# A decoder trunk on one core: additions moved to GpSimd between the layers, splits put ahead of moves, and a first x tile made without h

## What is computed

```python
for i in range(DEPTH):
    f = swiglu(rmsnorm(h, P['g_f1_pre'][i]), P['w_f1_gate'][i], P['w_f1_up'][i], P['w_f1_down'][i])
    h = h + 0.5 * rmsnorm(f, P['g_f1_post'][i])
    mo, a1, a2, a3 = mixer(rmsnorm(h, P['g_mix_pre'][i]), bpool[i], bsc[i], bcf[i], pos0, P, i)
    h = h + rmsnorm(mo, P['g_mix_post'][i])
    f = swiglu(rmsnorm(h, P['g_f2_pre'][i]), P['w_f2_gate'][i], P['w_f2_up'][i], P['w_f2_down'][i])
    h = h + 0.5 * rmsnorm(f, P['g_f2_post'][i])
    gate = jax.nn.sigmoid(rmsnorm(h, P['g_ple_pre'][i]) @ P['w_ple_gate'][i])
    h = h + rmsnorm((p[i] @ P['w_ple_proj'][i]) * gate, P['g_ple_post'][i])
```

## Time and profile before

| what | value |
|---|---|
| median of three runs | 1541.18 us |
| the three runs | 1539.96, 1541.18, 1541.54 us |
| the profiled execution's own time | 1541.55 us |
| its span in the trace | 1539.9 us |
| busy: TensorE | 1525.8 us (99%) |
| busy: VectorE | 1034.3 us (67%) |
| busy: ScalarE | 720.5 us (47%) |
| busy: GpSimd | 654.0 us (42%) |
| mean granted TensorE clock | 0.995 |

### The profile page before, as it was taken

How to read it: one execution, slowest core, us unless ns; L and a number is a source line. 1 busy time by engine, 2 the same in 40 slices (tenths; PEclk the granted TensorE clock), 3 DMA queues, 4 the chain that set the end, 5 groups by cost and what they waited for, 6 DMA issues and landing times.

```text
span 1539.9 us, 27992 instructions
## 1 busy us (share of the span) xinstructions
PE 1525.8 (99%) x10361; PEld 1518.3 (99%) x10361; DVE 1034.3 (67%) x1589; ACT 720.5 (47%) x1086; POOL 654.0 (42%) x695
## 2 busy tenths in 40 slices
PE   9999999999999999999999999999999999999997
PEld 9999999999999999999999999999999999999997
DVE  7655437999886755533885554389998866555347
ACT  6333336445466433433753334354554664334356
POOL 2855203499331565500147551045973307554012
PEclk9999999999999999999999999999999999999998
DMA  6545432444443544533334454334444335445422
GB/s 220 169 158 181 180 129 83 164 139 163 151 161 110 187 149 151 186 144 117 125 123 166 148 194 177 119 110 138 152 151 163 121 137 187 156 143 188 150 82 82
DMA packets 54281, 229.30 MB, mean 149 GB/s; under 512 B 3776, under 2 KB 6208, under 8 KB 49856
## 3 DMA queue, kind: packets, MB, share of 16 engines
q1 hardware_dynamic: 53632, 226.07, 42.9%
q10 hardware_dynamic: 576, 2.26, 0.4%
HBM read 225.27 MB, written 3.04 MB: 148 GB/s over the span
## 4 chain that ended last, share of the span: by engine, by line
PE 96%; issue 2%; DVE 1%; POOL 1%; ACT 0%; DVEq 0%; POOLq 0%; ACTq 0%
PE ps L504 29%; PE ps L506 29%; PE ps L505 29%; PE ps L546 2%; PE ps L542 2%; PE ps L543 2%; PE ps L668 1%; PE ps L580 1%; PE ps L572 1%; PE ps L571 1%; PE ps L617 0%; PE ps L609 0%; PE ps L636 0%; POOL x_lo L1765 0%; ACT win L1249 0%
## 5 line engine op out<-in xcount | busy, mean ns | idle before, releaser
L1271 DVE TENSOR_TENSOR w_lo_sb<-raw,w_hi_sb 128x1024 fp32r<-128x1024 f32 (+1 forms) x384 | 546.2, 1424 | 219.8 <-ACT w_hi_sb L903 218.9
L903 ACT ACTIVATE w_hi_sb<-raw 128x1024 fp32r<-128x1024 f32 (+1 forms) x384 | 424.7, 1112 | 546.6 <-PE ps L506 445.7
L504 PE MATMUL ps<-x_hi,w_hi_sb 128*128 128x320 f32 x2176 | 674.2, 310 | 0.8 <-DVE w_lo_sb L1271 0.8
L505 PE MATMUL ps<-x_lo,w_hi_sb 128*128 128x320 f32 x2176 | 671.9, 309 | 0.0
L506 PE MATMUL ps<-x_hi,w_lo_sb 128*128 128x320 f32 x2176 | 671.9, 309 | 0.0
L504 PEld LDWEIGHTS ps<-x_hi,w_hi_sb 128*128 128x128 f32 x2176 | 408.5, 188 | 2.7 <-issue 1.3
L505 PEld LDWEIGHTS ps<-x_lo,w_hi_sb 128*128 128x128 f32 x2176 | 408.6, 188 | 0.3
L506 PEld LDWEIGHTS ps<-x_hi,w_lo_sb 128*128 128x128 f32 x2176 | 408.5, 188 | 0.0
L506 PE MATMUL ps<-mid_hi,w_lo_sb 128*128 128x320 f32 x704 | 217.4, 309 | 0.0
L504 PE MATMUL ps<-mid_hi,w_hi_sb 128*128 128x320 f32 x704 | 217.4, 309 | 0.0
L505 PE MATMUL ps<-mid_lo,w_hi_sb 128*128 128x320 f32 x704 | 217.4, 309 | 0.0
(11 more groups left out here) (244 smaller groups left out, 1720.8 us busy)
## 6 DMA issues: line engine op xcount, KB each, us to landing
raw<-in_w_f_up SPq DMA_DIRECT2D x84, 1024.0 KB, 5.3
raw<-in_w_f_dn SPq DMA_DIRECT2D x32, 1408.0 KB, 5.9
raw<-in_w_gate SPq DMA_DIRECT2D x24, 1024.0 KB, 5.3
raw<-in_w_out SPq DMA_DIRECT2D x12, 1024.0 KB, 5.3
...
```

Source lines behind the costliest of these rows:

```text
L504: pe.matmul(out, whi, rhs_hi, start=start, stop=False, skip_group_check=True)
L505: pe.matmul(out, whi, rhs_lo, start=False, stop=False, skip_group_check=True)
L903: act.activation(w_hi_sb[:, j, 0:n], src[:, 0:n], ACT.Copy).then_inc(w_hi, 1)
L1271: dve.tensor_tensor(w_lo_sb[:, j, 0:n], src[:, 0:n], w_hi_sb[:, j, 0:n].bitcast(F32), ALU.subtract).then_inc(w_lo, 1)
```

## The change

It has four parts.

1. In f1_up of both layers the third pair's step is written out (`split_first_step`): each slot's split stands in front of the move, not behind it.
2. At boundaries 0, 1 and 2 of both layers the first x tile is made without h. ScalarE prepares f and h of tile 0 scaled by the gain ahead of time (`first_ahead`, into gb), and VectorE makes x from them with bc (`first_x`), and a second copy that GpSimd reads instead of ScalarE's. h of tile 0, still needed, is computed behind tile 4, and its square moves behind tile 4's. The order of h is now 1, 2, 3, 4, 0, 5, 6, 7 (`CHASE`).
3. Between the layers GpSimd adds the squares of tiles 0 to 6. TensorE's separate sums for tiles 5 and 6 go; the fillers there are 6, 3 and 3 in place of 4, 1, 1, 4 and 3. The splits of the next layer's first two slots change places with the operations around them.
4. At the end GpSimd multiplies a third chunk by the gain, which VectorE finishes last, and TensorE runs fillers between the sums of the chunks.

```diff
+        CHASE = (1, 2, 3, 4, 0, 5, 6, 7)
+        def h_at(n, m):
+            return (CHASE.index(m) if n < 3 else m) + 1
+        AHEAD_F, AHEAD_H = gb[:, 0, :], gb[:, 1, :]
...
                     if name == "post4":
-                        for m in POST4_ALONE:
-                            keep_warm(WARM_ALONE)
-                            pe.wait_ge(squared, v_sq(L, name, m))
...
-                        keep_warm(WARM_SIG)
+                        keep_warm(WARM_ROOT)
...
                 for i, (b, c) in enumerate(CHUNKS):
+                    for _ in range((6, 3, 3, 3, 0)[i]):
+                        pe.matmul(ps[:, 2, 0:T], pw_hi[:, 0:P], p_hi[:, 0:T], start=True, stop=True)
...
+            def first_ahead(L, n, gain):
+                c = cur[:, COL[gain]:COL[gain] + 1]
+                if n != 1:
+                    act.wait_ge(mid_ready, (L * 2 + (1 if n == 0 else 2)) * FT + 2)
+                act.wait_ge(f_out, v_f(L, n, 0))
+                act.activation(AHEAD_F, f[:, 0, :], ACT.Copy, scale=c).then_inc(ahead, 1)
+                act.activation(AHEAD_H, h[:, 0, :], ACT.Copy, scale=c).then_inc(ahead, 1)
...
-                    act.activation(CHASE_SQ[m - 1], h[:, m - 1, :], ACT.Square).then_inc(squared, 1)
+                    while done < DT and (order[done] < m and (n == 3 or order[done] or m > 4)):
+                        act.activation(CHASE_SQ[done], h[:, order[done], :], ACT.Square).then_inc(squared, 1)
+                        done += 1
...
-                    if nxt_layer and m in (5, DT - 1):
-                        split(*nxt_layer, 0 if m == 5 else 2)
+                    if nxt_layer and m == DT - 1:
+                        split(*nxt_layer, 2)
                     sigmoid(sg[:, m % RING3, :], ga[:, m % 2, :], L, "pg", m)
+                    if nxt_layer and m in (5, 6):
+                        split(*nxt_layer, m - 5)
...
+                def first_x():
+                    dve.wait_ge(ahead, (L * 3 + n) * 2 + 2)
+                    dve.tensor_tensor(steps[1], AHEAD_F, bc, ALU.mult).then_inc(x0_step, 1)
+                    dve.wait_ge(x0_step, L * 3 + n + 1)
+                    dve.tensor_tensor(x_hi[:, 0, :], steps[1], AHEAD_H, ALU.add).then_inc(x0_hi, 1)
+                    dve.tensor_tensor(SCALED_H[0], steps[1], AHEAD_H, ALU.add).then_inc(gh_ready, 1)
...
-                step(0)
-                new_h(0)
-                dve.wait_ge(h_ready, before + 1)
-                dve.tensor_scalar(x_hi[:, 0, :], h[:, 0, :], cur[:, g:g + 1], None, ALU.mult).then_inc(x0_hi, 1)
+                if n < 3:
+                    first_x()
...
                     if i - 1 not in POOL_X:
                         x_low(i - 1)
+                    if n < 3 and i == 4:
+                        step(0)
+                        new_h(0)
...
+            def split_first_step(L, ph):
+                for j in range(4):
+                    split(L, ph, 2, j)
+                    dve.wait_ge(halves_done, v_half(L, ph, 1, j) + 4)
+                    if j % 2 == 0:
+                        dve.wait_ge(mid_ready, L * 2 * FT + 2 + j // 2 + 1)
+                    move((ga, gb)[j % 2][:, j // 2, :], j)
...
                 dve.wait_ge(ple_out, L * DT + DT)
+                dve.wait_ge(summed, v_sq(L, "post4", DT - 3))
...
-            for i in (2, 3, 4):
+            for i in (3, 4):
                 b = CHUNKS[i][0]
                 dve.scalar_tensor_tensor(HT[i], HT[i], rinv[:, b:b + 1], G_ROW[i], ALU.mult, ALU.mult).then_inc(y_dve, 1)
+            dve.wait_ge(hg_ready, 3)
+            b = CHUNKS[2][0]
+            dve.tensor_scalar(HG[2], HG[2], rinv[:, b:b + 1], None, ALU.mult).then_inc(y_dve, 1)
...
                 if L + 1 < DEPTH:
+                    for m in range(DT - 1):
+                        wait_alone(squared, v_sq(L, "post4", m))
+                        if m == 0:
+                            pool.tensor_copy(ssq[:, 0:T], sq[:, 0, :]).then_inc(summed, 1)
+                        else:
+                            wait_alone(summed, v_sq(L, "post4", m - 1))
+                            pool.tensor_tensor(ssq[:, 0:T], ssq[:, 0:T], sq[:, m % 2, :], ALU.add
+                                               ).then_inc(summed, 2 if m == DT - 2 else 1)
                     boundary_x(L, 3)
```

82 lines of the change are left out of this document (46 added, 36 removed).

## The result

The changed kernel takes 1543.35 us (median of 20 runs, 1541.54 to 1544.90), the kernel before beside it 1541.11 (20 runs, 1539.74 to 1541.58). The ratio is 1.0016, with an interval of 1.0010 to 1.0022: 2.2 us longer, still within 0.2%. The forecast was 1542.5. The profiled execution has a span of 1542.3 us and a time of 1543.92, against 1539.9 and 1541.55 before; its busy times, which answer to the earlier trace rows, are

A forecast was written before the change was run, and what follows sets the result against it. TensorE, busy 99% of the span, was taken to bound the kernel. 4.8 - 0.8 - 2.4 - 0.3 = +1.3 us on 1541.18 gave 1542.5, range 1537.8 to 1545.2; the forecast had a chance of 0.66.

The forecast's parts named there:

- part 1: Third pair of f1_up: TensorE's 0.82 us wait in layer 0 goes, gain 0.8 (0 to 1.0); layer 1, 0.
- part 2: Three boundaries of each layer: h of tile 0 delays later tiles, 4.8 us lost (3.0 to 6.5).
- part 3: Between the layers: last sums start 2.3 after the dense work if VectorE is in time; gain 2.4 (1.5 to 3.0).
- part 4: The end: shorter last product and fillers between chunks, gain 0.3 us (-0.3 to 0.7).
- delay of 1.39: At the boundaries: x of tiles 6 and 7 later by 0.93 on VectorE plus 0.46 for a second ScalarE square.
- forecast of 0.7 a layer: Boundary 0: tile 6's low part, with slack 0.79, loses 0.60; 0.7 put for the place (0.3 to 1.39).
- third rival: Between the layers: GpSimd's additions hold VectorE up, last sums 1.86 later, part 3 gives 0.5; +3.2, 1544.4; chance 0.09.
- possible 1.5: Between the layers: 1.0 + 0.5 us on top if TensorE's clock stays up, nearly none if it falls; 0.9 taken.
- prediction's own sign: The prediction is wrong if boundaries show no new wait, or if the passage between the layers is no shorter.
- Covered tiles: Boundaries: ScalarE and VectorE catch up before tile 6, so late tiles cost nothing; 1537.5, faster; chance 0.13.
- the whole delay: Boundaries: slack used up at all six places, each costs 1.39; +4.8, 1546.0, slower; chance 0.12.
- the change doesn't do what it says: First boundary: step_t holds GpSimd back, tile 0's low part 0 to 0.3 us later; already in the sum.

The follow-up runs named there:

- experiment 1: Kernel before with part 2 alone (parts 1, 3 and 4 undone): 1543.99 us against 1540.92, ratio 1.0020.
- experiment 6: Changed kernel with fourteen fillers, not six, between the layers, and h of tile 0 behind tile 7, its square last: 1538.60 us, ratio 0.9986.
- experiment 7: Changed kernel with fourteen fillers between the layers, without GpSimd's own wait for the first step at boundary 0: 1542.17 us, ratio 1.0010.
- experiment 9: Changed kernel with fourteen fillers, h of tile 0 last and no GpSimd wait for the first step at boundary 0: 1538.17 us, ratio 0.9982.
- experiment 2: Changed kernel without part 2 (three boundaries as before; parts 1, 3 and 4 kept): 1539.25 us, ratio 0.9991.
- experiment 3: Kernel before with part 3 alone: 1540.80 us, ratio 0.9997.
- experiment 8: Changed kernel with fourteen fillers, GpSimd's six additions between the layers cut to 64 of 320 columns: 1541.35 us, ratio 1.0004.
- experiment 12: Experiment 9 with GpSimd adding tiles 0 to 4 only, TensorE summing 5 and 6, and 5, 1, 1 and 1 fillers: 1539.31 us, ratio 0.9991.
- experiment 4: Changed kernel with fourteen fillers in place of six ahead of the sums between the layers: 1542.05 us, ratio 1.0004.
- 11: Experiment 9 without part 3, the passage between the layers and its fillers as before the change: 1539.46 us, ratio 0.9991.

## Why the prediction was right, and where it was wrong

The sign was right, and so was the size, within 0.2%: +2.2 where +1.3 was forecast. That it came so near is in part luck: the two largest terms were off in opposite directions, by 1.3 and by 2.5 us.

| term | forecast | measured in the trace |
|---|---|---|
| start (chance) | 0 | -0.15 |
| part 1, layer 0 | -0.8 | -0.53 |
| part 1, layer 1 | 0 | -0.26 |
| part 2 | +4.8 (3.0 to 6.5) | +3.5 |
| part 3 | -2.4 (-1.5 to -3.0) | +0.15 |
| part 4 | -0.3 | -0.4 |
| sum | +1.3 | +2.4 |

*Part 1.* Right in mechanism. The next late thing was named, the move; it was taken to be just in time and is 0.28 late, because the split in front of it took 1.89 and not 1.48. In layer 1, where 0 was put because the list names no wait, the same place gives 0.26: in the trace of before a product follows the one ahead of it there by 0.30 (797.88 to 798.18) where 0.15 is usual, without a wait in the list, and with the clock up the wait is named (experiment 1). So the total of 0.8 is right by luck.

*Part 2.* The mechanism, h of tile 0 in the middle of the queues, is what experiment 6 takes away, and the cost goes with it. The delay of 1.39 measured 1.15 at tile 6: 0.91 on VectorE as forecast, but only 0.25 more from the second square, not 0.46. At boundary 0 the forecast of 0.7 a layer had the right size (0.87 and 0.90; 0.97 and 0.55 in experiment 1) in part at the wrong place: in layer 0 0.55 fall at the boundary and 0.33 in the mixer. Of the 0.55 about 0.3 arise already at tile 0's low part, which the prediction saw coming later and left out of the sum, and 0.2 at tile 6, where 0.60 was expected; experiment 7 shows that tile 6 alone would have taken both. In the mixer the chain of VectorE and GpSimd runs about 0.3 behind its old times from the boundary on (the reciprocal of the norm starts at 263.27, before at 262.93), and TensorE, at first still 0.13 ahead of its own, meets it some 100 us later. This was read from the traces, not tried by itself; with h last boundary 0 and the mixer together still cost 0.25 (experiments 6 and 9), and without part 2 nothing (experiment 2). At boundary 1 the forecast was that the delay runs on to the third pair of f2; that place shows no loss, and the 0.37 arise at tile 6. In layer 1 the 0.03 there are against an execution of before that lost 0.35 at that place by itself: experiments 2 and 3, which leave this boundary as it was, both show -0.35. At boundary 2 of layer 0 1.3 were forecast and 0.88 measured, 0.30 of it TensorE's named wait for the sum. That a gain of the first tile would not come off was right for this kernel, and the reason is sharper than the one given: even with tile 6 in time, tile 2's low part stands where it stood.

*Part 3.* This is the step that failed. It said that the last sums come 2.3 after the dense work, by the last layer's row, if VectorE is in time. VectorE was not: it was done with the square of tile 7 3.47 after the dense work, no sooner than before (3.39). The product of tile 6 took 1.17 beside an addition, and a split of 1.21 stood between it and the last move. This is the third rival's mechanism, to which 0.09 was given, at the place it named; the measured time lies between the forecast and its 1544.4. Experiments 8 and 12 settle it: 0.61 beside a short addition, 0.48 beside none; and with short additions all along the square is done at 2.25, where the forecast had 2.24. The hold is 1.2, not the rival's 1.86. The Trainium skill (SBUF — State Buffer, Who interferes with whom) says that a VectorE instruction with two SBUF inputs and a GpSimd instruction that reads SBUF exclude each other. The traces here agree, with 1.17 and 1.05 against 0.48. The row for it was there before the change: GpSimd's own products, 1.66 and 0.93 in the earlier trace rows. In the trace of before the slower kind takes 1.69 on average in the 84 places where a split runs beside it and 0.88 in the other four; the prediction's "elsewhere" for the 0.93 doesn't hold, since nearly all of these stand beside a split too. What was wrong was to call the additions hidden because GpSimd had time for them.

The second half of that step was the clock. It took 0.9 of a possible 1.5, as if the stretch at the lower clock would become shorter. It began 4.8 after the end of the dense work, 3.4 before, kept its length, and lay on dense work instead. Nor is there a gain from the work itself where the clock stays up (experiments 1 and 4, told of under 11). By the prediction's own sign, a passage that is no shorter, this part of it is wrong. No row of one trace of before could show that the stretch is there in one execution and absent in the next; the spread of the three runs (1539.96 to 1541.54) was the only hint, and it was read as noise.

*Part 4* was right.

*The rivals.* Covered tiles (1537.5) are refuted by experiment 1, the whole delay (1546.0) by the table. That the change doesn't do what it says, at the first boundary, held: GpSimd's low part waits for tile 1's step there. Experiment 7 shows that even so it costs nothing, as long as tile 6 is later still.
